# Who makes the low half of the second plain gate's weights: GpSimd beside the first norm tiles, or VectorE in two halves around the last one

## The reference, cut to what matters

```
h2 = rmsnorm(x, norm2_g) * (1 + sc2) + sh2
a, b = split(dwconv3(h2 @ w_up, ffn_conv_w), 2)      # w_up: 1024 x 5632, conv of width 3 along the tokens
x = x + g2 * ((silu(a) * b) @ w_down)
```

## Time and profile before

| | us |
|---|---|
| median of 3 runs | 1567.98 (1566.52 to 1570.54) |
| the profiled execution's own time | 1567.95 |
| its span in the profile | 1566.1 |
| TensorE matmul busy | 1549.9 (99%) |
| VectorE busy | 1046.8 (67%) |
| ScalarE busy | 726.9 (46%) |
| GpSimd busy | 188.3 (12%) |
| mean granted TensorE clock | 0.995 of full |

### The profile page before, as it was taken

One profiled execution on the slowest core, in us unless ns is written; L12 is line 12 of the kernel. 1 busy time (PEld: TensorE's weight loads), 2 busy tenths in 40 slices (PEclk: granted clock), 3 DMA queues, 4 the chain that ended last, 5 costly groups with the idle time before them and its releaser, 6 DMA issues.

```text
span 1566.1 us, 26388 instructions
## 1 busy us (share of the span) xinstructions
PE 1549.9 (99%) x10573; PEld 1456.5 (93%) x10573; DVE 1046.8 (67%) x1661; ACT 726.9 (46%) x1218; POOL 188.3 (12%) x197
## 2 busy tenths in 40 slices
PE   8999999999999999999999999999999999999998
PEld 6778899998999999999987788899899999999998
DVE  6763767738785855858777447685688677486683
ACT  5444444326652634626454344542565355263462
POOL 1000000004202202113000000000221120130210
PEclk9999999999999999999999999999999999999999
DMA  9653011475756846659453501033367584584752
GB/s 361 244 174 136 28 54 37 156 240 138 179 142 141 199 127 160 163 146 201 155 183 127 202 28 55 28 109 108 95 145 165 137 186 132 149 192 134 181 140 85
DMA packets 278366, 225.63 MB, mean 144 GB/s; under 512 B 9674, under 2 KB 253700, under 8 KB 278244
## 3 DMA queue, kind: packets, MB, share of 16 engines
q1 hardware_dynamic: 259680, 189.89, 38.1%
q0 software_dynamic: 18320, 33.96, 12.8%
q10 hardware_dynamic: 244, 0.09, 0.0%
HBM read 188.78 MB, written 3.67 MB: 123 GB/s over the span
## 4 chain that ended last, share of the span: by engine, by line
PE 96%; DVE 2%; DMA 1%; ACT 1%; SPq 0%; issue 0%; DVEq 0%; ACTq 0%
PE ps L1185 11%; PE ps L1187 11%; PE ps L1189 11%; PE ps L1242 7%; PE ps L1244 7%; PE ps L1243 7%; PE ps L739 4%; PE ps L740 4%; PE ps L741 4%; PE ps L894 4%; PE ps L895 3%; PE ps L896 3%; PE ps L1034 3%; PE ps L1061 3%; PE ps L1101 3%; PE ps L1102 2%
## 5 line engine op out<-in xcount | busy, mean ns | idle before, releaser
L1638 ACT ACTIVATE w_hi<-raw_all 128x1024 fp32r<-128x1024 f32 x120 | 126.3, 1058 | 203.1 <-PE ps L1244 100.0
L1242 PE MATMUL ps<-gg,w_hi 128*128 128x322 f32 x704 | 218.5, 310 | 0.0
L1244 PE MATMUL ps<-gg,w_lo 128*128 128x322 f32 x704 | 218.2, 310 | 0.0
L1243 PE MATMUL ps<-gg,w_hi 128*128 128x322 f32 x704 | 218.1, 310 | 0.0
L1187 PE MATMUL ps<-hc_lo,w_hi 128*128 128x322 f32 x640 | 199.5, 312 | 0.0
L1185 PE MATMUL ps<-hc_hi,w_hi 128*128 128x322 f32 x640 | 199.0, 311 | 0.0
L1189 PE MATMUL ps<-hc_hi,w_lo 128*128 128x322 f32 x640 | 198.6, 310 | 0.0
L2235 DVE TENSOR_TENSOR w_lo<-raw_all,w_hi 128x1024 fp32r<-128x1024 f32 x120 | 147.7, 1230 | 72.4 <-ACT w_hi L1638 70.2
L678 POOL DMA_DIRECT2D raw_all<-raw_all x120 | 102.6, 860 | 552.6 <-DMA raw_all<-in_w_up_dram 481.0
L2196 DVE SCALAR_TENSOR_TENSOR tmp<-ub,vecs,tmp 128x642 f32<-128x642 f32 x168 | 140.9, 883 | 15.2 <-ACT tmp L1596 13.7
L2130 DVE SCALAR_TENSOR_TENSOR x<-ps,modv,x 128x128 f32<-128x128 f32 (+2 forms) x240 | 90.4, 434 | 89.8 <-PE ps L1244 54.3
(11 more groups left out here) (236 smaller groups left out, 3549.0 us busy)
## 6 DMA issues: line engine op xcount, KB each, us to landing
raw_all<-in_w_up_dram SPq DMA_DIRECT2D x280, 256.0 KB, 4.0
raw_all<-raw_all POOLq DMA_DIRECT2D x120, 256.0 KB, 3.9
raw_all<-in_w_in_dram SPq DMA_DIRECT2D x48, 512.0 KB, 6.9
mod_p<-in_w_mod_dram SPq DMA_DIRECT2D x20, 1024.0 KB, 7.3
raw_all<-in_w_down_dram SPq DMA_DIRECT2D x16, 768.0 KB, 4.4
raw_all<-in_w_down_dram SPq DMA_DIRECT2D x16, 640.0 KB, 4.1
mod_q<-in_w_mod_dram SPq DMA_DIRECT2D x8, 1024.0 KB, 9.2
raw_all<-in_w_out_dram SPq DMA_DIRECT2D x16, 512.0 KB, 4.3
```

The lines of the kernel that those rows point to most:

```text
L1242: mm(out, wh[:, k, :], gh, start=k == 0, stop=False)
L1243: mm(out, wh[:, k, :], gl, start=False, stop=False)
L1244: ins = mm(out, wl[:, k, :], gh, start=False, stop=k == kf - 1)
L1638: A(whi_b[:, 2 * i:2 * (i + 1), :], src, ACT.Copy).then_inc(up_hi[i], 1)
```

## The change

GpSimd no longer makes the low half of gate 6's weights, and its two waits go too. VectorE makes it in two halves of 128x1024: the first at i = 9 of the norm loop, just ahead of the low half of the last tile, the second right behind the loop and ahead of `mod_post`. `split_full[1]` is now signalled by the second half.

```diff
@@ GpSimd's stream
-                pool.wait_ge(hi_done[1], l * SPLIT_SLOT + (G_U + 1) // 2 + 1)
-                pool.wait_ge(diag_ready, 3 * NT * (l + 1))
-                nc.gpsimd.tensor_tensor(w_lo[:, 1, :], raw[:, 1, :], w_hi[:, 1, :].bitcast(F32), ALU.subtract
-                                        ).then_inc(split_full[1], 1)
@@ VectorE's stream
+                def held_lo(half):
+
+                    w = slice(half * (SLOT // 2), (half + 1) * (SLOT // 2))
+                    dve.wait_ge(hi_done[1], l * SPLIT_SLOT + (G_U + 1) // 2 + 1)
+                    ins = V.tensor_tensor(w_lo[:, 1, w], raw[:, 1, w], w_hi[:, 1, w].bitcast(F32), ALU.subtract)
+                    if half:
+                        ins.then_inc(split_full[1], 1)
+
                 for i in range(KT + 2):
...
+                    if i == KT + 1:
+                        held_lo(0)
                     if i >= 2:
...
+                held_lo(1)
                 mod_post(l, GAP_A[l] + 1)
```

## The result

The changed kernel takes 1575.86 us (median of 6 runs, 1574.12 to 1578.57), the kernel before 1568.73 in the same comparison: 1.0049 times as long, 95% interval 1.0038 to 1.0059. That is 7.1 us slower by the medians (7.7 by the ratio); the forecast was 1567.4 with 1571.0 as the upper end. It was wrong in sign and size. The true cause, the late sums, stood among its rivals with a price too small.

A forecast was written before the change was run, and what follows sets the result against it. It took TensorE, with matmuls filling 99% of the span, to bound the kernel. Terms: -0.6 (layer 0's first hc_lo) + 0 (layer 1) + 0 + 0 = -0.6 us, giving 1567.4; range 1565.0 to 1571.0.

The forecast's parts named there:

- the late sums: Rival: adds beside seven loads make gate 1's sums late, overrunning ScalarE's string; 1569.4, up to 1571.0; chance 0.28.
- Part 1, the removal: Layer 0's first hc_lo drops from 1.63 to 0.83 us; 0.18 lost at the second tile; gain 0.6 us.
- The later tiles: Gate 0's later feature tiles come at less than 1.78 us each, so they count at nothing.
- Part 2, VectorE's work: Two 128x1024 subtractions around the last norm tile, 2.46 us per layer at most, fit VectorE's room: cost 0.
- Part 3, the loads behind the signal: SyncE's nine loads go 12.9 us later; gate 1's sums still fit: cost 0, bounds 0 to 0.2 us per layer.
- The hold of GpSimd's DMAs by VectorE: Skill's rule: GpSimd-issued DMAs wait for descriptors during VectorE's two-port mode; weighed against part 3, not seen in the trace.
- Over 2 us more: VectorE's half of gate 1's string, ending with product 4's split, has over 2 us more room than ScalarE's.
- It regains that there: Gate 2's loads wait for the late sums too, but gate 2, 12.4 us behind gate 1, regains the delay.
- Late by 4 us in both layers: Rival: the load chain comes late by 4 us in both layers, -0.6 + 8 = 1575.4; chance 0.04.
- A difference that can't be told: Result within 0.3% (4.7 us) of the kernel before, covering all cases but the last; chance 0.91.
- 0.7 us of room: Room left at gate 1's product 2 before late sums delay it: 0.15 us on ScalarE plus 0.57 behind.

The follow-up runs named there:

- e10: Kernel before, GpSimd's subtraction cut to 8 of its 2048 columns, nothing in its place: 1567.71 us, ratio 1.0004.
- e2: Kernel before, two unused 128x1024 subtractions added to VectorE where the change has them, loads released as before: 1567.18 us, ratio 1.0000.
- e8: Changed kernel, VectorE's two halves moved ahead of the norm loop: 1569.27 us, ratio 1.0000 to the kernel before.
- e5: Changed kernel, SyncE waiting for gate 1's first sum after loading blocks 7 and 8: 1579.89 us, ratio 1.0069 to the kernel before.
- e4: Changed kernel, five of the nine block loads issued ahead of the signal: 1567.56 us, ratio 1.0006 to the kernel before.
- e1: Kernel before, each layer's first block loads held until VectorE's eighth low half of the norm tiles: 1569.23 us, ratio 1.0014.
- e11: Kernel before, first block loads held until the mod_post behind the norm loop, no added VectorE work: 1567.98 us, ratio 1.0008.
- e9: Changed kernel, VectorE waiting in gate 1 until GpSimd's add of gate 2 is done: 1575.71 us, ratio 1.0054 to the kernel before.
- e7: Kernel before, GpSimd's subtraction no longer waiting for the norm's factors (diag_ready): 1577.38 us, ratio 1.0053.
- e3: Kernel before, VectorE's two added subtractions plus first block loads held until the mod_post behind them: 1576.10 us, ratio 1.0064.

## Why the prediction was wrong, point by point

**Part 1, the removal: right.** The first `hc_lo` took 0.83 us, the second 0.92 with 0.30 of waiting ahead, as in layer 1 before. In this profile gate 0 started only 0.24 us earlier, since TensorE's granted clock was down to 0.50 (the lower of the two levels that the rows show, 0.50 and 1.00) at 356 to 358 us, while it spread the factors; that comes and goes between profiles. Counted from VectorE's first `hfull`, gate 0 began after 3.84 us in place of 4.64: the 0.80 that was forecast. e10's interval runs from a gain of 0.6 us to a loss of 2.0: nothing measurable, in keeping with the 0.6. (The later tiles do not all come within 1.78 us, as the prediction has it: in the kernel before, the fourth low half started 2.63 us after the third, around a short turn of TensorE's. No wait came of it.)

**Part 2, VectorE's work: right.** e2 and e8 show 0. The last tile's low half was there at 373.8, the signal at 374.97.

**Part 3, the loads behind the signal: the step that failed.** Its chain was the right one, and its sizes were too small: the first sum was forecast at 383.5 and came at 387.06. Forecast, then measured, in layer 0: blocks 7 and 8 at the add 3.6 us after the signal, 5.6; the first add 5.2, 6.5 (380.55 to 387.06); the second 4.3, 3.25. Part of this could be read off the rows of before. The 3.2 us for block 8 is the median of two loads that fell into that window, block 7's 2.9 and block 8's own 3.6; in the changed kernel it took 4.6. GpSimd started the add 0.5 us after the landing, which the sum leaves out, and of the first add's 6.5 us some 0.3 is the step from landing to GpSimd's next instruction, which the 3.5 against 3.2 of before shows. For the add beside loads I had taken two rows of steady state (5.2 and 4.9), where a few loads were under way; here seven stood in the queue. e5, e4 and the changed kernel give the dose: 3.2, 4.4, 6.2 us beside none, three, seven. With an upper bound of 5.2 twice the range could not hold this. The hold of GpSimd's DMAs by VectorE, which the prediction weighed against this part, did not show: e5's add landed in 3.2 us, as the one of before did, with VectorE at work beside it.

**"Over 2 us more" for VectorE: wrong.** VectorE's half of the string had less room than ScalarE's. In e1 and e11, with the first sum at 21.8 us in layer 0, ScalarE still stood 0.97 and 0.96 us for the end of gate 6, as the prediction wants it, and yet VectorE's third split was 1.3 us late. The forecast's own first sum, 383.5, is 21.7 us on that scale. So with every size of the chain right, part 3 would still have cost something like e11's 1.3 or e1's 2.2 us.

**"It regains that there": wrong, and the dearer error.** I let gate 2 start afresh because it comes 12.4 us behind gate 1. But SyncE loads gate 2's blocks 4 and 5 when gate 1's third split has left them; that split stood 4.0 us later (398.62 for 394.60), so the load was issued at 399.86 instead of 395.85, the add of block 4 at 404.13 instead of 399.49, ScalarE's copy at 407.66 instead of 403.50, and `s1` of gate 2 at 410.59 instead of 407.05, where TensorE had about half a us to spare. The rows of before:

```profile
399.49 0.84 POOL L678 DMA_DIRECT2D raw_all<-raw_all  x1 [9.15 <-DMA raw_all<-in_w_up_dram]
```

```profile
403.50 1.06 ACT L1638 ACTIVATE w_hi<-raw_all 128x1024 fp32r<-128x1024 f32 x1 [2.26 <-DMA raw_all<-raw_all]
...
407.05 0.42 ACT L1656 ACTIVATE s<-ps 128x322 f32<-128x322 f32 x1
```

I had given this split "over 2 us more" because its own product came later. I had looked for its reader on TensorE and not for the one on SyncE. Of the 5.6 us of waits for `s1` only 0.93 are gate 1's; the other three are gate 2's and 3's. That this step makes them is read from the rows; no run cut it by itself.

**What made the string rigid.** When the first sum is late, VectorE and ScalarE run their string behind it nearly back to back, and a GpSimd add gets in between: the low half of T2 took 2.63 us and not 1.49 beside the add at 390.31. (In the kernel before the same add, at 379.46, stretched a combination of VectorE's from 1.50 to 2.60; there VectorE had 3.97 us of idle time ahead of the third split, so it cost nothing.) Whether the lock-out of GpSimd by VectorE (2.86 and 3.73 us for an add of 1.3) adds to the price was asked of e9: taking it away brought nothing, since the add of block 4 landed nearly as late.

**The chances.** The rival "sums come late" had 0.28 and was priced up to 1571.0, for a second sum at 390.3. The second sum came at 390.3 to the tenth; it was the price that was wrong, since it counted only the wait in gate 1. "Late by 4 us in both layers", 1575.4, had 0.04. That is the measured time within 0.5 us, and the split was late by 4.2 and 3.2 us, but no chain led to this number, so it is partly luck. A difference that can't be told had 0.91; the 7.1 us are beyond the prediction's own bound of 4.7. My own central value left 0.7 us of room in a chain of six terms, three of them read off rows of another load; such a margin is no margin, and the case should have had at least even odds.

**What stays open.** Why the second of the two blocks took 4.6 us to land in layer 0 of the changed kernel and of e5, and 3.1 to 3.3 in their layer 1 and in e1: in e5 the DMA engines were nearly idle (0.04) from 378.0 us, so the other loads are not it. And the waits for `s1` make 5.6 of the 7.5 us by which the span grew. Another 0.7 lie ahead of gate 0 in layer 1: TensorE's granted clock was 0.50 there from 1122 to 1126 us, its 32 matmuls ahead of gate 0 took 2.98 us in place of 1.91, and gate 0 began at 1127.72, 0.67 us after its first low half was ready. e10 and e7 show a late start in layer 1 too (0.42 and 0.68 us), so it is not put down to the change. The remaining 1.2 us I can't assign row by row (restarts show first matmuls of 0.41 us in place of 0.31).

## What to carry to other kernels

An operation that is moved takes its signal with it, so list all readers of the semaphore, above all a DMA queue, and treat the loads behind it as moved by the same time. For each late item ask who reuses its buffer, not only who computes with it: gate 2 gave none of gate 1's delay back here, because the release of its buffers was itself late. If the signal has to come late, first take from behind it what doesn't need it: five of nine loads here, and the whole loss was gone.

## What the runs showed of the hardware that was not expected

- An accumulating DMA from SBUF to SBUF (256 KB, issued by GpSimd) landed 3.2 us after issue alone (e5, both layers), 4.4 and 3.7 beside three 256 KB loads from HBM (e4), 6.2 and 5.8 beside seven (changed kernel; 5.4 to 7.0 in the other kernels with seven).
- GpSimd's subtraction with two SBUF inputs held up VectorE's `tensor_scalar` with a single SBUF tensor input too: 4.95 us for five that take 1.07 (e7). The Trainium skill, page "SBUF — State Buffer", section "Who interferes with whom", counts `tensor_scalar` among what can contend, in its two-port mode; e7 agrees that it was held up, and no run shows the mode. Without GpSimd's wait for the norm's factors the kernel before is 8.8 us slower.
- Beside an unbroken string of VectorE instructions a GpSimd add of 1.3 us took 2.86 and 3.73 us in the changed kernel and 3.93 and 3.66 in e3, with VectorE's instructions beside it at 1.2 us or less; with VectorE stopped for it (e9) it took 1.98 and 1.78.
